# Plain high and low blocks for queries and gate rows, two late sigmoids and eight more idle turns

## The reference

```python
shift, scale, gate = jnp.split(mod, 3, axis=-1)
h = rmsnorm(x, rms_g) * (1 + scale) + shift
q, k, v, z_a, glu, z_b, gates = jnp.split(h @ w_in + b_in, PROJ_SPLITS, axis=-1)
y_a = attend(q, k, v) * jax.nn.silu(z_a)
y_b = conv_branch(glu, dw_w, dw_b, ln_g, ln_b) * jax.nn.silu(z_b)
g_a, g_b = jnp.split(jax.nn.sigmoid(gates), 2, axis=-1)
m = g_a * (y_a @ w_proj_a) + g_b * (y_b @ w_proj_b)
return x + gate * (m @ w_out), k, v
```

## Time and profile before

| | |
|---|---|
| three runs | 1723.14, 1723.22, 1723.63 us; median 1723.22 |
| profiled execution | 1724.99 us, its span 1723.4 us |
| PE | 1701.1 us busy, 99% of the span, 9909 matmuls |
| PEld, DVE, ACT, POOL | 1442.6, 1242.2, 862.1, 653.6 us busy |
| DMA | 286.31 MB, 166 GB/s over the span |
| granted clock of PE | 0.998 over the span, 9 tenths or more in every fortieth of it |

### The profile page before, as it was taken

The page is one execution under the profiler, slowest core; times in us unless marked ns, Lnnn a source line. Parts: engine busy times, 40 slices in busy tenths (PEclk is TensorE's granted clock), DMA queues, the critical chain, the costliest instruction groups (busy, mean ns, idle before and its releaser), DMA issues.

```text
span 1723.4 us, 27674 instructions
## 1 busy us (share of the span) xinstructions
PE 1701.1 (99%) x9909; PEld 1442.6 (84%) x9909; DVE 1242.2 (72%) x1789; ACT 862.1 (50%) x1501; POOL 653.6 (38%) x509
## 2 busy tenths in 40 slices
PE   8999999999999999999999999999999999999998
PEld 5787888888899988888888888889898888888886
DVE  3785888788757858888687856777777665677776
ACT  3553434455567644434544437777779222333443
POOL 0044675565200026856555653224223100005443
PEclk9999999999999999999999999999999999999999
DMA  9443534333598734444333368988666777673442
GB/s 325 126 150 126 135 124 143 93 92 110 178 309 262 211 96 129 155 132 111 98 127 100 104 172 219 230 205 209 167 146 172 247 231 234 191 261 134 148 158 86
DMA packets 271644, 286.31 MB, mean 166 GB/s; under 512 B 49960, under 2 KB 217748, under 8 KB 268309
## 3 DMA queue, kind: packets, MB, share of 16 engines
q1 hardware_dynamic: 271106, 284.18, 56.0%
q10 hardware_dynamic: 403, 0.37, 0.1%
HBM read 203.18 MB, written 81.30 MB: 165 GB/s over the span
## 4 chain that ended last, share of the span: by engine, by line
PE 86%; DMA 4%; DVE 3%; issue 2%; POOL 2%; ACT 1%; SPq 1%; POOLq 0%; ACTq 0%; DVEq 0%
PE banks L1837 38%; PE banks L2391 6%; PE banks L2965 4%; PE banks L2967 4%; PE banks L2966 4%; DMA w_raw<-in_w_in 3%; PE banks L3025 3%; PE banks L3027 3%; PE banks L3026 3%; PE banks L2355 2%; PE banks L1967 2%; PE banks L1966 2%; PE banks L1965 2%; PE banks L2361 2%; PE banks L2331 1%
## 5 line engine op out<-in xcount | busy, mean ns | idle before, releaser
L1837 PE MATMUL banks<-a_hi,w_hi 128*128 128x512 f32 x1176 | 460.2, 391 | 0.8 <-ACT out_stage L1117 0.4
L1837 PE MATMUL banks<-a_hi,w_lo 128*128 128x512 f32 x1176 | 457.8, 389 | 0.0
L1837 PE MATMUL banks<-a_lo,w_hi 128*128 128x512 f32 x1176 | 457.7, 389 | 0.0
L1506 DVE SCALAR_TENSOR_TENSOR banks<-glu_out,taps,banks 128x1009 f32<-128x1009 f32 (+1 forms) x240 | 342.2, 1426 | 5.2
L1837 PEld LDWEIGHTS banks<-a_hi,w_hi 128*128 128x128 f32 x1176 | 220.8, 188 | 50.0 <-issue 3.6
L1837 PEld LDWEIGHTS banks<-a_hi,w_lo 128*128 128x128 f32 x1176 | 220.8, 188 | 46.4
L1837 PEld LDWEIGHTS banks<-a_lo,w_hi 128*128 128x128 f32 x1176 | 220.9, 188 | 45.0
L1006 POOL TENSOR_TENSOR t_raw<-w_raw 128x512 f32<-128x512 f32 x39 | 53.6, 1373 | 400.6 <-DMA w_raw<-in_w_in 394.4
L1425 DVE SCALAR_TENSOR_TENSOR w_lo<-w_raw,w_hi 128x1024 fp32r<-128x1024 f32 x84 | 108.9, 1296 | 104.9 <-ACT w_hi L1097 103.6
L960 POOL TENSOR_TENSOR w_lo<-t_raw,w_hi 128x1024 fp32r<-128x1024 f32 x70 | 171.6, 2461 | 23.7 <-ACT w_hi L1097 21.4
L2503 ACT ACTIVATE probs<-scores,stat 128x640 f32<-128x640 f32 (+2 forms) x128 | 106.6, 833 | 51.2 <-DVE stat L2425 49.8
(11 more groups left out here) (282 smaller groups left out, 3678.6 us busy)
## 6 DMA issues: line engine op xcount, KB each, us to landing
w_raw<-in_w_in SPq DMA_DIRECT2D x34, 1024.0 KB, 5.7
cw_raw<-in_w_in SPq DMA_DIRECT2D x44, 512.0 KB, 5.0
proj<-out_stage SPq DMA_DIRECT2D x80, 256.0 KB, 2.3
gates_in<-proj SPq DMA_DIRECT2D x64, 256.0 KB, 3.0
k_hi<-k_hi_rows SPq DMA_DIRECT2D x16, 640.0 KB, 11.5
k_lo<-k_lo_rows SPq DMA_DIRECT2D x16, 640.0 KB, 13.5
q_split<-q_rows SPq DMA_DIRECT2D x8, 1152.0 KB, 6.0
w_ada<-in_w_ada SPq DMA_DIRECT2D x8, 1024.0 KB, 11.2
```

Source lines behind the costliest of these rows:

```text
L1506: op = dve.scalar_tensor_tensor(dst, src, by, dst, ALU.mult, ALU.add)
L1837: op = pe.matmul(out, x[w][:, b, k], y, start=(start and k == j == 0), stop=(k == H - 1 and j == 2), skip_group_check=not start)
```

## The change

Four edits in one:

1. `keep_busy(41)` becomes `keep_busy(49)` in front of the first turns of x.
2. `q_rows` becomes [hi/lo, 512, token] and `z_rows` [half, 512, token]. Each store of a part is one DMA of 128 rows; each load of a head is two DMAs of 64 rows. Counts of the waits follow (`qk_in` 96, `z_in` 32 a head).
3. Part C21 of `LAST_A` and `LAST_B` is stored without its Sigmoid.
4. In the merge ACT applies the Sigmoid to the loaded gates: `late_gate`, for chunks 3 and 4 of the merge and output blocks 4 and 6, on 256 tokens each, and DVE waits for it before the second branch's product.

```diff
+        n = 16
...
+            count = 2 if za or kind == "sv" else 0 if role in ("full", "sig") else 1
...
-    io.q_rows = nc.dram_tensor("q_rows", (HEADS, 2, DH, TOK), F32, kind="Internal").ap()
+    io.q_rows = nc.dram_tensor("q_rows", (2, WA, TOK), F32, kind="Internal").ap()
...
-    io.z_rows = nc.dram_tensor("z_rows", (HEADS, 2, DH, TOK // 2), F32, kind="Internal").ap()
+    io.z_rows = nc.dram_tensor("z_rows", (2, WA, TOK // 2), F32, kind="Internal").ap()
...
             if kind == "q":
-                head = (col - Q0) // DH
-                for j in range(2):
-                    sp.dma_start(io.q_rows[head + j, i, :, tok], stg_r[DH * j:DH * j + DH, slot].bitcast(F32)).then_inc(out_d[slot], 16)
+                sp.dma_start(io.q_rows[i, col - Q0:col - Q0 + P, tok], stg_r[:, slot].bitcast(F32)).then_inc(out_d[slot], 16)
...
                 if kind == "q":
-                    head = (col - Q0) // DH
-                    for e in range(2):
-                        sp.dma_start(io.q_rows[head + e, j, :, LAT:TOK], xo_r[DH * e:DH * e + DH, h].bitcast(F32)).then_inc(xo_d[h], 16)
+                    sp.dma_start(io.q_rows[j, col - Q0:col - Q0 + P, LAT:TOK], xo_r[:, h].bitcast(F32)).then_inc(xo_d[h], 16)
...
-            act.activation(part_ap(q, "C21"), result_ap(q, banks[:, q % 2]), func_of(kind), bias=bias_of(kind, cols[0])).then_inc(copied, 1)
+            func = ACT.Identity if q >= LAST_A else func_of(kind)
+            act.activation(part_ap(q, "C21"), result_ap(q, banks[:, q % 2]), func, bias=bias_of(kind, cols[0])).then_inc(copied, 1)
...
-        keep_busy(41)
+        keep_busy(49)
...
         def load_queries(n):
             u = n % 2
-            sp.dma_start(q_sp[u][:].bitcast(F32), io.q_rows[n].rearrange("h p t -> (h p) t")).then_inc(qk_in[u], 16)
+            for h in range(2):
+                sp.dma_start(q_sp[u][DH * h:DH * h + DH].bitcast(F32), io.q_rows[h, DH * n:DH * n + DH]).then_inc(qk_in[u], 16)
...
-            sp.dma_start(z_sb[:, n % 2], io.z_rows[n].rearrange("h p t -> (h p) t")).then_inc(z_in[n % 2], 16)
+            for h in range(2):
+                sp.dma_start(z_sb[DH * h:DH * h + DH, n % 2], io.z_rows[h, DH * n:DH * n + DH]).then_inc(z_in[n % 2], 16)
...
+LATE_GATES = [(c, (PAIRS[q][1] - G0) // P - 8) for c in (3, 4) for q in (LAST_A, LAST_B)]
...
+    def late_gate(act, c, o):
+
+        og = 8 * c + o
+        act.wait_ge(g_in[og % 3], g_base[og % 3] + 32 * (og // 3 + 1))
+        g = gate_buffer(og)[:, 1, 256 if c == 3 else 0:512 if c == 3 else 256]
+        act.activation(g, g, ACT.Sigmoid).then_inc(late_done, 1)
...
+            if branch == 0 and (c, o) in LATE_GATES:
+                late_gate(act, c, o)
...
+            if branch and (c, o) in LATE_GATES:
+                dve.wait_ge(late_done, LATE_GATES.index((c, o)) + 1)
```

More of the change, by code:

```diff
@@ L169, in c_slot @@
     return {"C11": 0, "C21": 1, "C22": 2, "C12": 3 + q % 2}[part]
-def stores_of(kind, col):
-    return 2 if kind == "q" or kind == "z" and col < ZA0 + WA else 1
 def part_order():
@@ L255, in front_plan @@
         col = PAIRS[q][1 + PART[part][0]]
-        n = 16 * stores_of(kind, col)
+        n = 16
         wants_hi = kind in ("q", "k") and how == "post" or kind == "v" and how == "copy"
@@ L310, in context_plan @@
             za = kind == "z" and BLOCKS[n][1] < ZA0 + WA
-            count = 4 if za else 2 if kind in ("q", "sv") else 0 if role in ("full", "sig") else 1
+            count = 2 if za or kind == "sv" else 0 if role in ("full", "sig") else 1
             p.total[h] += 16 * count
@@ L672, in store_part @@
             if kind == "z" and col < ZA0 + WA:
[L673 to L676, removed]
+                sp.dma_start(io.z_rows[c % 2, col - ZA0:col - ZA0 + P, 512 * (c // 2):512 * (c // 2) + 512],
+                             stg[:, s]).then_inc(out_d[s], 16)
             else:
@@ L751, in store_unit @@
         elif kind == "z" and col < ZA0 + WA:
[L752 to L756, removed]
+            for t in range(2):
+                sp.dma_start(io.z_rows[t, col - ZA0:col - ZA0 + P, LAT // 2:TOK // 2], xo[:, h, P * t:P * t + P]
+                             ).then_inc(xo_d[h], 16)
         else:
@@ L2322, in scores @@
             if m % TPH == 0:
-                pe.wait_ge(qk_in[n % 2], 80 + 80 * (n // 2))
+                pe.wait_ge(qk_in[n % 2], 96 + 96 * (n // 2))
             if m >= 2:
@@ L2454, in gate_out @@
             if at == 0:
-                dve.wait_ge(z_in[n % 2], 16 * (n // 2 + 1))
+                dve.wait_ge(z_in[n % 2], 32 * (n // 2 + 1))
                 if n >= 2:
@@ L2714, in tail @@
     first_act, first_done, first_hid, first_lod = (sem(n) for n in ("first_act", "first_gated", "first_hid", "first_lod"))
-    const_in, act_pair = sem("const_in"), sem("act_pair")
+    const_in, act_pair, late_done = sem("const_in"), sem("act_pair"), sem("late_gates")
     mm2, sc_done, z_done, sq_done, r_done, fin_done = (sem(n) for n in ("out_mm", "scaled", "z_done", "z_sq", "z_rs", "y_fin"))
```

## The result

The changed kernel takes **1725.74 us**, median of 19 runs (1723.98 to 1728.9), against 1723.28 (1722.33 to 1727.55, 19 runs) for the kernel before on the same chip: a ratio of 1.0013, 95% interval 1.0007 to 1.0019, that is 1.2 to 3.3 us more. The prediction was 1721.6, with 1719.9 to 1723.9 as its range. The time moved the other way and left the range. Of all executions reported here one, of run e11, took 2113.94 us at a granted clock of 0.752, and that run's ratio leaves it out.

The account below looks back on a forecast made before the run. TensorE, busy 1701.1 of 1723.4 us, bounds the kernel, so only its 22.3 us of gaps count. Terms 0 - 1.2 - 0.4 + 0 + 0 = -1.6 on the median 1723.22 give 1721.6 us, range 1719.9 to 1723.9.

Parts of the forecast that it names:

- the loads: Attention heads: 16 more query and gate-row loads are covered by slack before the values of head 1; 0, bounds 0 and +0.5.
- the stores: Context stage near 517 us: fewer store issues free DVE's half slot sooner; -1.2 us, bounds 0 and -1.63.
- rival B: Attention heads: half loads run at half rate, values of head 1 wait up to 7.7 us, 1729.3 us; chance 0.04.
- The gate rows of head 0: First attention head: two loads instead of one may land 0.3 us later, before TensorE's turn at 1050.74; covered.
- rival A: Context stage and seam: nothing moves, same bytes through full queues; 1722.8 to 1723.6 us, chance 0.18.
- both gaps: Context stage: TensorE waits of 0.68 us at 520.10 and 0.95 at 531.64; first to go, second to lose 0.5.
- The idle turns: Start: eight more turns cost at most 1.23 us, covered; clock gain up to 1.7 us dies later; 0, bounds +0.3 and -1.7.
- 12.2 was the mark: Start: sign that the 55 turns end before 12.2 us in the changed profile.
- the landings: Start: w_ada tiles landing at 25.37 and 40.68 and x_rows at 46.07 absorb any earlier gain of up to 1.7 us.
- The seam: Projection to attention near 1043 us: without a Sigmoid table load, exponents begin 0.45 us sooner; -0.4 us, bounds 0 and -0.5.
- The merge: End of the merge: four Sigmoids and five table loads on ACT delay DVE, but not TensorE; 0.
- the tight gate: Merge, second gate of the fourth chunk: ready at 1488.85, wanted by DVE at 1488.28, 0.6 us late.

Follow-up runs that it names:

- e11: Kernel before with only the last two gates changed (Identity in the projection, Sigmoid in the merge), timed a second time: 1723.90 us, ratio 1.0005.
- e6: Kernel before with only the new layout, stores of 128 rows and loads of 2 x 64 rows; idle turns and gates as before: 1723.98 us, ratio 1.0005.
- e12: The changed kernel itself, timed again beside the kernel before: 1725.24 us, ratio 1.0007.
- e15: Changed kernel with the queries of a head in four loads of 32 rows instead of two of 64: 1724.81 us, ratio 1.0006 to the kernel before.
- e5: Kernel before with query and gate-row loads split in two by columns, 128 rows in each: 1722.92 us, ratio 0.9998.
- e8: Changed kernel without its storage part: 49 idle turns and gates in the merge, old stores and loads: 1723.83 us, ratio 0.9999 to the kernel before.
- e3: Kernel before with 49 idle turns at the start instead of 41, nothing else: 1723.42 us, ratio 1.0000.
- e4: Kernel before with only the last two gates as Identity in the projection and Sigmoid in the merge: 1722.71 us, ratio 0.9996.
- e13: Changed kernel with queries and gate rows in one load of 128 rows each, from wrong rows: 1723.92 us, ratio 0.9999 to the kernel before.
- e9: Changed kernel with 41 idle turns instead of 49, storage part and gates kept: 1724.55 us, ratio 1.0009 to the kernel before.

## Why the prediction was wrong, by its own steps

Two terms of the sum were wrong, the loads (0 given, 1.4 us measured) and the stores (1.2 us of gain given, none found). The first made the changed kernel slower; the second made the forecast lower than it should have been.

**The loads: the step that failed.** I gave them 0 with bounds 0 and +0.5, on two grounds. The first was that three issues more, 1.35 us, meet a slack of 1.3, with 2.4 us for a landing. In the trace of before the last landing for head 1 stands at 1079.57, so the slack was 2.2. The second was the comparison of the earlier trace rows: 1152 KB in 128 rows land in 6.0 us, 640 KB in 64 rows in 11.5 "but those queue behind the queries". I read no rate from it, and put the half rate aside as rival B with 0.04. The window of before at 1056 (401 GB/s, then 206 for the keys) showed it in the trace that I had. Two halves of the queries need 2 x 576 KB at 224 GB/s = 5.3 us where one full load needs 2.9 at 401, gate rows half of that: 3.5 us more ahead of the values. The sync engine stands behind the full queues, and from its issue of the gate rows to that of the last value load 23.6 us go by instead of 1076.19 - 1055.68 = 20.5. All traces agree: from the issue of the queries of head 1 to the last landing of its values pass 26.9 to 29.0 us in the eight with loads of 128 rows (before among them) and 29.9 to 32.5 in the seven with half loads, 2.5 more in the mean.

The issues in after:

```profile
1055.55 1.24 SPq L2272 DMA_DIRECT2D z_halves<-z_rows  x2
1056.83 21.87 SPq L2242 DMA_DIRECT2D v_win<-v_tokens  x16
1078.75 0.39 SPq L2243 DMA_DIRECT2D v_ctx<-in_cache_v  x1
1079.18 0.47 SPq L2244 DMA_DIRECT2D v_ctx<-v_tokens  x1
```

The last load is issued at 1079.18 instead of 1076.19, TensorE is 0.6 us earlier, and it waits 1.18. Rival B named this mechanism and place. Its price of 7.7 us was too high, since it took the 6.0 us from issue to landing for transfer time and doubled that; about half of it is the delay before a load's bytes move.
The gate rows of head 0, "one load issued at 1045.16 and used at 1049.39", I called covered with 0.3 us for a second load. In e6, e12 and e15 DVE waits 1.38 to 1.83 us for them and TensorE 0.7 to 1.2. From the first issue to the last landing these rows take 4.0 to 5.4 us with 128 rows (4.1 in e5, with its two loads) and 5.1 to 5.9 with 64, 1.0 more in the mean where I had 0.3. The step failed for the same reason.

**The stores: -1.2 forecast, nothing of it found.** The mechanism was wrong, and rival A's fits. In after SP issues two query stores in 0.94 us instead of four in 2.86, and the next store pays, so that the key store behind them is handed over at 513.60 instead of 514.18 (the last row is of before):

```profile
509.27 0.94 SPq L726 DMA_DIRECT2D q_rows<-ctx_stage_r  x2
510.25 0.57 SPq L640 DMA_DIRECT2D cw_raw<-in_w_in  x1
510.87 2.73 SPq L729 DMA_DIRECT2D k_hi_rows<-ctx_stage_r  x1
...
513.00 1.18 SPq L740 DMA_DIRECT2D k_hi_rows<-ctx_stage_r  x1
```

Behind that key store 0.58 of the 1.92 us are left. DVE's wait is 2.97 us, and both gaps are there:

```profile
520.36 0.66 PE L1743 MATMUL banks<-ident,x_rows 128*128 128x128 f32 x4 [1.02 <-DVE ctx_stage_r L1548]
...
531.89 0.63 PE L1743 MATMUL banks<-ident,x_rows 128*128 128x128 f32 x4 [0.95 <-issue]
```

Nor are they a fixed property of a kernel: with the old stores, e8 has both, e3 the second alone, and e4 and e5 only 0.3 to 0.4 us at the second. From 470 to 620 us TensorE's waits add up to 0.4 to 2.6 us in the nine traces with stores of 128 rows (1.2 in the mean) and to 0.7 to 2.2 in the seven with 64 (1.4). A gain of some tenths can hide in that, 1.2 us hardly.

**The idle turns: 0, right.** 55 turns end at 11.56 (12.2 was the mark), the granted clock at 14 us is 1.00, the upper level (the last section says why this is not shown to be the turns' work), the 16 products take 1.92 us instead of 3.62, and the landings take it back: the wait before 49.14 ends as at 49.13 in before.

```profile
3.57 7.99 PE L1698 MATMUL banks<-ident 128*128 128x128 f32 x55
...
13.95 1.92 PE L1710 MATMUL banks<-w_ada,silu_wide 128*32 128x512 f32 x16 [0.57 <-DMA w_ada<-in_w_ada]
...
49.14 0.50 PE L1750 MATMUL banks<-a_hi,fw_hi 128*128 128x512 f32 x1 [0.79 <-DVE a_lo L1392]
```

**The seam: -0.4, right in the trace.** The wait is 0.52 instead of 0.94, and DVE's reduction at 1043.71 is what exponents wait for:

```profile
1043.71 0.08 DVE L2415 DVE_READ_ACCUMULATOR2_ANT stat<- 128x1 f32 x1
...
1043.83 0.83 ACT L2493 ACTIVATE probs<-scores,stat 128x640 f32<-128x640 f32 x1 [0.88 <-DVE stat L2415]
```

**The merge: 0, right.** DVE waits 0.60 us for the tight gate, close to the 0.57 worked out, and no TensorE wait follows:

```profile
1487.75 1.28 ACT L3143 ACT_TABLE_LOAD   x1
1489.05 0.42 ACT L3143 ACTIVATE gates_in<-gates_in 128x256 f32<-128x256 f32 x1
1489.48 1.28 ACT L3040 ACT_TABLE_LOAD   x1
```

```profile
1489.59 0.69 DVE L3363 TENSOR_TENSOR gated_b<-banks,gates_in 128x512 f32<-128x512 f32 x1 [0.60 <-ACT gates_in L3143]
```

The Silu load starts 0.01 us behind the Sigmoid's end and the Sigmoid 0.02 behind its own load. So the drain of 1.38 us of the Trainium skill's page (ScalarE: Activation LUTs, "What ACT_TABLE_LOAD costs") stands behind neither of these loads, and the price of a switch here is 1.28.

**The sum and the chances.** By the steps as measured, -1.6 becomes +1.0: -0.4 at the seam, 0 for the stores, +1.4 for the loads in the changed kernel's trace. The median moved by 2.46, interval 1.2 to 3.3, and 1.0 lies just below that. So of the 4.1 us between the forecast of 1721.6 and the 1725.74 measured, the loads account for 1.4 and the stores for 1.2, and 1.5 stay open. They may be scatter, which is not shown; against the kernel beside it the changed kernel stood at +1.9 by the medians when timed again (e12), 0.0 without the half loads (e13).
The range failed for want of the half rate. 3.5 us more of queue against the slack of 2.2 gives +1.3; with the stores at their bound of 0 that makes 1723.2 - 0.4 + 1.3 = 1724.1, beyond the 1723.9 that was the upper end. The chance of 0.04 for B went by its price of 7.7 us; the same mechanism at 1.3 us had no rival of its own.

## What to carry to other kernels

Before a load is split, read the rate at which it moves: a window in which nothing else is under way, with its GB/s and rows per load. Count the bytes of everything queued ahead of the tile that is needed next, at that rate, and compare that with the slack; the issue time of a DMA behind full queues is no measure of either. Where medians scatter by as much as the effect, compare a stretch between two events that every kernel has: here it told 1.0 us with single traces, where eleven executions did not.

## What the runs showed that I had not expected

A load whose source has the two blocks as its outermost dimension made the kernel 236 us slower than before (e2). The Trainium skill (DMA: Bandwidth & Descriptors, "Why a DMA increments its semaphore by 16 and not by 1") says that a copy is spread over the largest number of engines, up to 16, that divides the slowest dimension of both sides, so over two here. The window at 1100 us agrees: a busy share of 0.13 of 16 engines is 2.1 engines, at 52 GB/s.
The granted clock near 14 us is not set by the number of turns alone. In e9, which has 41, it is 1.00 (2.4 GHz) after an idle time of 1.50 us, in e6 0.54 (near 1.2 GHz) after 1.40, as before after 1.44. Of the nine traces with 41 turns seven show 1.00 there, and so do all eight with 49, so that no effect of the eight turns on the clock is shown.

```profile
13.90:17.60 3.70, 3.29 (x27) 1.62 (x28) 0.71 (x2) 1.04 (x2) 0.00 (x0) 1.00 1.09 342
```

```profile
13.90:17.60 3.70, 3.53 (x17) 0.68 (x18) 0.17 (x2) 0.94 (x1) 0.00 (x0) 0.54 1.09 343
```
